# Output projection with three weight slots and passes of 2, 3 and 3 token tiles; the first product's high parts ahead, TensorE kept busy before it

## The chip, the core and the metric
One core of one Trainium2 chip runs the whole program. The metric is the device time of one execution in microseconds (us), median of the runs; lower is better.

## The reference, cut to what matters
One encoder layer on 1024 tokens of width 1024, in float32:
```
x = x + 0.5 * rmsnorm((silu(h @ w1_gate) * (h @ w1_up)) @ w1_down, g)      # h = rmsnorm(x)
z = rmsnorm(x) @ w_in                                                       # pool channels, q, k, v
a = concat(pool_mixer(z), dilated_window_attention(z))                      # 1024 tokens x 1024
x = x + rmsnorm(a @ w_out, g_mix_post)                                      # the output projection
x = x + 0.5 * rmsnorm((silu(h @ w2_gate) * (h @ w2_up)) @ w2_down, g)       # h = rmsnorm(x)
```

## The kernel before
Every large product splits each float32 operand into a high part (rounded to fp32r, made by ScalarE with a copy) and a low part (the rest, made by VectorE with a subtraction), and adds three products on TensorE: high by high, high by low, low by high. So each weight piece passes ScalarE, then VectorE, then TensorE. The engines run fixed instruction lists written by hand, each in its own order, joined by semaphore waits; a wait in one list holds all that stands behind it in that list.

Stages, in order: gate/up of the first feed-forward half (`gate_up(0)`), its down product (`down(0)`), input projection with attention, output projection (`project_out`), `gate_up(1)`, `down(1)`. A token tile is 128 tokens; there are NT = 8, four to a half (HT).

**Start of a gate/up stage.** Tiles 0 to 3 are normalised (`x_norm`), turned by TensorE (`turn_x`, 8 transposes), and their turned form is split: `x_hi` and `x_copy` on ScalarE, `x_lo` on VectorE. Three tail products (`tail_product`, X, Y and Z, 24 matmuls of 128x512 each) come first; their weights are split by `hi_tail` and `lo_tail`. Between them TensorE turns tiles 4 to 7 (`turn_second`), which VectorE takes apart in `split` (one subtraction in two pieces, then two sums) and `s_14` (two more sums). Then come the 12-matmul products (`product`) in the order of FIRST_M: (0,0), (1,0), (0,4), (1,4), where the first number is the weight unit, and after them three more tail products, which need all four `split`. The weights of unit 0 and 1 are 1 MB loads by SyncE, which start once `lo_tail` of Y and of Z are done. `first_steps` holds these lists for ScalarE and VectorE.

**End of a gate/up stage.** `combine` and `times_up` on VectorE finish the stage, `lo_d(0)` and `lo_d(1)` make the low parts of the first two steps of the down product; TensorE's first down step waits for `lo_d(0)`.

**Output projection.** For a pass of token tiles, TensorE runs 8 units, one for each 128 rows of `w_out`; a unit is 6 matmuls of 128x512 for each tile of the pass. The passes are `OUT_TILES`, (0,1,2), (3,4,5), (6,7): 18, 18 and 12 matmuls a unit. For each unit `hi_proj` (ScalarE, 128x1024 and 128x384 or 128x256) and `lo_proj` (VectorE, the same shapes) split weights and activations, into one of two slots; a slot is free when the unit two before is done. In the first pass the activations are only just made: TensorE turns the attention's output (`turn_outputs`), ScalarE and VectorE copy it. Before unit 1 the softmax coefficients go through TensorE, and GpSimd scales the outputs with them (`scale_out`, L518).
Beside the units, each finished tile i takes a chain of small steps, whose places in the order `OUT_SIDE` fixes (the unit index n is counted through all 24): copy out of PSUM (`evac_mix`), square sum (`sq1`), GpSimd's root, `scale_y` and `x_new` on VectorE, store and next load and `sq2` on ScalarE, GpSimd's root, `x_norm` on VectorE, and for tiles 0 to 3 `turn_x`, `x_hi`, `x_copy`, `x_lo`:
```
OUT_SIDE = {7: 0, 10: 1, 13: 2, 16: 3, 18: 4, 20: 5}
...
for base, i in OUT_SIDE.items():
    if n == base:
        sq1(R_MIX + i, junk_f[:, :], mixed)
    if n == base + 2:
        x_store(R_MIX + i)
        x_load(R_MIX + i + 2)
        sq2(Q_FFN[1] + i, junk_f[:, :])
```
`x_store` waits on ScalarE for `x_new` of its tile. Tiles 6 and 7 are left for `last_mixed`.

## Time and profile before
| | |
|---|---|
| median of 3 runs | 1762.67 us (1762.55 to 1763.8) |
| the profiled execution | 1763.64 us, its span 1761.2 us |
| TensorE busy | 1708.9 us, 97% of the span |
| VectorE, ScalarE, GpSimd busy | 1117.0, 711.6, 628.6 us |
| mean granted TensorE clock | 0.991 |

The span runs from the first to the last instruction; the rest of the execution, 2.4 us, lies around it. An engine's busy time counts the union of its instructions.

### The profile page before, as it was taken

What the parts mean: (1) busy time and instruction counts of PE and PEld (TensorE: products, weight loads), DVE (VectorE), ACT (ScalarE), POOL (GpSimd) and SP (SyncE); (2) the same over time, 40 slices, a digit from 0 to 9 for tenths busy, and PEclk for the clock granted to TensorE, in tenths of its full rate; (3) what the DMA queues carried; (4) which work ended last, traced back from release to release, by engine and by line L of the source; (5) the groups of instructions that cost most, each with busy time, mean ns of one, the idle gap of its engine ahead of it and who ended that gap; (6) DMA issues with size and microseconds to landing.
All of it is one profiled execution on the core that took longest, in us unless ns stands there. A gap on an engine that the chain in (4) does not pass through costs nothing.

```text
span 1761.2 us, 21622 instructions
## 1 busy us (share of the span) xinstructions
PE 1708.9 (97%) x7918; PEld 1403.7 (80%) x7918; DVE 1117.0 (63%) x1403; ACT 711.6 (40%) x1256; POOL 628.6 (36%) x494
## 2 busy tenths in 40 slices
PE   6999999999999999999999999899999999999997
PEld 5888888888788878887888787688888888788886
DVE  6775665565668784424556658877665655557877
ACT  6433323332444553433444456533333333244453
POOL 3354554553453111108010201246554544445111
PEclk8999999999999999999999899999999999999999
DMA  6142224323853445332110156422233233384362
GB/s 209 42 133 95 90 91 130 115 90 104 315 186 98 142 150 162 113 97 84 49 50 23 49 167 202 130 87 90 90 111 135 90 104 104 141 294 147 101 228 90
DMA packets 160984, 216.97 MB, mean 123 GB/s; under 512 B 12848, under 2 KB 99056, under 8 KB 160880
## 3 DMA queue, kind: packets, MB, share of 16 engines
q1 hardware_dynamic: 153136, 188.73, 33.6%
q10 hardware_dynamic: 6896, 24.19, 3.9%
q0 software_dynamic: 848, 2.69, 0.5%
q8 instruction: 63, 1.03, 0.2%
q14 instruction: 41, 0.34, 0.1%
HBM read 162.09 MB, written 52.95 MB: 122 GB/s over the span
## 4 chain that ended last, share of the span: by engine, by line
PE 88%; DVE 6%; ACT 3%; issue 2%; POOL 1%; ACTq 0%; DMA 0%; DVEq 0%; POOLq 0%
PE ps L1960 15%; PE ps L1959 14%; PE ps L1961 14%; PE ps L2022 7%; PE ps L2024 7%; PE ps L2023 7%; PE ps L2052 4%; PE ps L2054 4%; PE ps L2053 4%; PE ps L2162 2%; PE ps L2270 1%; PE ps L2272 1%; PE ps L2271 1%; PE ps L2130 1%; PE ps L1917 1%
## 5 line engine op out<-in xcount | busy, mean ns | idle before, releaser
L1960 PE MATMUL ps<-xg,ring 128*128 128x512 f32 x1120 | 440.1, 393 | 0.0
L1959 PE MATMUL ps<-xg,ring 128*128 128x512 f32 x1120 | 437.7, 391 | 2.0 <-DVE u_a L1280 1.8
L1961 PE MATMUL ps<-xg,ring 128*128 128x512 f32 x1120 | 437.8, 391 | 0.0
L1959 PEld LDWEIGHTS ps<-xg,ring 128*128 128x128 f32 x1120 | 210.2, 188 | 51.3 <-DVE ring L1140 2.2
L1960 PEld LDWEIGHTS ps<-xg,ring 128*128 128x128 f32 x1120 | 210.4, 188 | 45.0
L1961 PEld LDWEIGHTS ps<-xg,ring 128*128 128x128 f32 x1120 | 210.4, 188 | 44.7
L2022 PE MATMUL ps<-ring 128*128 128x512 f32 x616 | 240.6, 391 | 2.7 <-DVE ring L1152 2.7
L2023 PE MATMUL ps<-ring 128*128 128x512 f32 x616 | 239.8, 389 | 0.0
L2024 PE MATMUL ps<-ring 128*128 128x512 f32 x616 | 239.7, 389 | 0.0
L683 ACT ACTIVATE ring<-t_sum 128x512 fp32r<-128x512 f32 x160 | 100.4, 630 | 290.1 <-PE ps L1961 162.1
L1159 DVE TENSOR_TENSOR ring<-raw,ring 128x1024 fp32r<-128x1024 f32 x64 | 84.6, 1322 | 154.8 <-ACT ring L705 129.7
L1673 POOL TENSOR_TENSOR t_sum<-raw 128x512 f32<-128x512 f32 x80 | 112.9, 1431 | 148.0 <-DVE ring L1140 132.2
L1140 DVE TENSOR_TENSOR ring<-t_sum,ring 128x512 fp32r<-128x512 f32 x160 | 151.5, 956 | 21.3 <-ACT ring L683 21.3
L1640 POOL TENSOR_SCALAR ms<-ss 128x1 f32<-128x1 f32 x44 | 20.7, 471 | 349.4 <-ACT junk_d L742 113.1
L1695 POOL TENSOR_TENSOR u_a<-hst 128x512 f32<-128x512 f32 x40 | 66.4, 1659 | 204.5 <-DVE hst L1269 204.5
L2022 PEld LDWEIGHTS ps<-ring 128*128 128x128 f32 x616 | 115.6, 188 | 28.5 <-DVE ring L1152 4.7
L1149 DVE TENSOR_TENSOR ring<-st_op,ring 128x1024 fp32r<-128x1024 f32 x66 | 103.9, 1575 | 51.3 <-ACT ring L694 51.1
L2024 PEld LDWEIGHTS ps<-ring 128*128 128x128 f32 x616 | 115.6, 188 | 24.1
L2023 PEld LDWEIGHTS ps<-ring 128*128 128x128 f32 x616 | 115.6, 188 | 23.9
L1140 DVE TENSOR_TENSOR ring<-raw,ring 128x512 fp32r<-128x512 f32 x120 | 126.6, 1055 | 5.7 <-ACT ring L683 5.7
L2052 PE MATMUL ps<-xe,ring 128*128 128x512 f32 x320 | 128.6, 402 | 0.0
L2054 PE MATMUL ps<-xe,ring 128*128 128x512 f32 x320 | 125.6, 393 | 0.0
(209 smaller groups left out, 2795.1 us busy)
## 6 DMA issues: line engine op xcount, KB each, us to landing
st_op<-hd_dram SPq DMA_DIRECT2D x154, 256.0 KB, 2.6
raw<-in_w_gate_dram SPq DMA_DIRECT2D x20, 1024.0 KB, 6.5
raw<-in_w_up_dram SPq DMA_DIRECT2D x20, 1024.0 KB, 5.4
raw<-in_w_in_dram SPq DMA_DIRECT2D x40, 512.0 KB, 3.9
hd_dram<-u_b SPq DMA_DIRECT2D x64, 256.0 KB, 6.4
wd<-in_w_down_dram SPq DMA_DIRECT2D x18, 768.0 KB, 7.3
hd_dram<-hst SPq DMA_DIRECT2D x48, 256.0 KB, 6.4
raw<-in_w_out_dram SPq DMA_DIRECT2D x24, 512.0 KB, 3.6
```

What stands on the lines that cost most here:

```text
L683: act.activation(small(m % RING, 0), src, ACT.Copy).then_inc(hi_done, 4 if m == M_FRONT - 1 else 1)
L1140: dve.tensor_tensor(small(m % RING, 1), src, small(m % RING, 0).bitcast(F32), ALU.subtract)\
L1149: a = dve.tensor_tensor(lo, src, hi.bitcast(F32), ALU.subtract)
L1673: pool.tensor_tensor(t_tile(n, t), x, y, ALU.subtract).then_inc(t_done, 1)
L1959: pe.matmul(acc, hi[:, a, :], x_hi, start=(a == 0 and not more), stop=False, skip_group_check=more)
L1960: pe.matmul(acc, hi[:, a, :], x_lo, start=False, stop=False, skip_group_check=more)
L1961: mm = pe.matmul(acc, lo[:, a, :], x_hi, start=False, stop=(a == HALF_D - 1), skip_group_check=more)
L2022: pe.matmul(acc, s_hi, w_hi, start=(j == 0 and not top), stop=False, skip_group_check=top)
L2023: pe.matmul(acc, s_hi, w_lo, start=False, stop=False, skip_group_check=top)
L2024: return pe.matmul(acc, s_lo, w_hi, start=False, stop=(j == PAIRS - 1), skip_group_check=top)
L2052: pe.matmul(ps[:, bank, :], hi[:, a, :], x_hi, start=(a == 0), stop=False)
L2054: mm = pe.matmul(ps[:, bank, :], lo[:, a, :], x_hi, start=False, stop=(a == DT - 1))
```

## The change
1. The start: VectorE makes all four norms before the first `x_lo`; ScalarE puts the tail weights between tiles and all but one `x_copy` behind; TensorE gets 6, 8, 3 and 14 extra transposes of the identity into unused banks (`fill`). Tail product X runs as 8 high by high matmuls, 8 low by high, 8 high by low, waiting for the low parts only where they come in; its first wait is for high parts alone. Other PSUM banks go with it.
2. Both `first_steps`: on VectorE `split(0)` moves behind `lo_g(1)`, and all `s_14` behind `lo_g(5)`; product (1,0) on TensorE now waits for `split(1)`.
3. Both ends of gate/up: `lo_d(0)` and `lo_d(1)` move ahead of `combine(4)`.
4. The output projection: passes (0,1), (2,3,4), (5,6,7), three slots instead of two, tables of places in place of `OUT_SIDE`; three tiles instead of two are left to `last_mixed`; the tail weights X and Y are split by ScalarE before the last unit. GpSimd starts the loads of the two gains after the last attention values instead of the last scores. For buffers this costs g_post_r and g_pre_r new places in SBUF (72 and 76 KB).

```diff
@@ -60,7 +60,7 @@
...
-TAIL_BANK = {(X_T, 0): 5, (Y_T, 0): 4, (Z_T, 0): 5, (Z_T, 1): 1, (X_T, 1): 5, (Y_T, 1): 1}
+TAIL_BANK = {(X_T, 0): 7, (Y_T, 0): 6, (Z_T, 0): 7, (Z_T, 1): 1, (X_T, 1): 5, (Y_T, 1): 1}
@@ -81,7 +81,7 @@
...
-TURN1_BANK, TURN2_BANK = (4, 0, 2, 6), (2, 6, 2, 6)
+TURN1_BANK, TURN2_BANK = (6, 0, 2, 4), (2, 0, 2, 6)
@@ -115,7 +115,7 @@
...
-OUT_TILES = [(0, 1, 2), (3, 4, 5), (6, 7)]
+OUT_TILES = [(0, 1), (2, 3, 4), (5, 6, 7)]
@@ -131,7 +131,12 @@
...
-OUT_SIDE = {7: 0, 10: 1, 13: 2, 16: 3, 18: 4, 20: 5}
+OUT_SQ1, OUT_NEW, OUT_SQ2 = (7, 9, 16, 17, 19), (8, 10, 17, 18, 20), (9, 11, 18, 19, 21)
+OUT_NORM, OUT_TURN = (10, 12, 19, 20, 22), (12, 14, 21, 22)
+EARLY = len(OUT_SQ1)
+FILL, FILL_BANK = (6, 0, 8, 3, 14), (5, 5, 5, 5, 6)
@@ -399,7 +404,7 @@
...
-            return (u - IN_U0[0]) % 2
+            return (u - IN_U0[0]) % 2 if u < OUT_U0 else (u - OUT_U0) % 3
@@ -701,10 +703,17 @@
...
                 act.wait_ge(p_loaded[k % RAW_SLOTS], 16 * (k // RAW_SLOTS + 1))
-                act.wait_ge(used, D0[0] + D_STEPS - 2 + k if k < 2 else u - 1)
+                if u < OUT_U0 + 2:
+                    act.wait_ge(used, D0[0] + D_STEPS - 2 + k if k < 2 else u - 1)
+                elif u == OUT_U0 + 2:
+                    act.wait_ge(pool_step, POOL_STEPS)
+                    act.wait_ge(s_done, NTILES)
+                else:
+                    act.wait_ge(used, u - 2)
                 a = act.activation(big(out_slot(u), 0), raw[:, k % RAW_SLOTS, :], ACT.Copy)
                 if src is not None:
-                    a = act.activation(hs_out[0][:, k % 2, 0:src.shape[-1]], src, ACT.Copy)
+                    a = act.activation(hs_out[0][:, out_slot(u), 0:src.shape[-1]], src, ACT.Copy)
                 a.then_inc(hi_done, 1)
@@ -1063,30 +1075,31 @@
...
-                    for base, i in OUT_SIDE.items():
-                        if n == base:
+                    for i in range(HT):
+                        if n == OUT_TURN[i]:
+                            x_hi(Q_FFN[1] + i, 6)
+                            x_copy(Q_FFN[1] + i, 6)
+                    for i in range(EARLY):
+                        if n == OUT_SQ1[i]:
...
-                        if n == base + 2:
+                        if n == OUT_SQ2[i]:
...
-                        if i < HT and n == base + 5:
-                            x_hi(Q_FFN[1] + i, 6)
-                            x_copy(Q_FFN[1] + i, 6)
-                    if n == 3 * OUT_UNITS - 3:
-                        hi_tail(1, X_T)
+                    if n >= 3 * OUT_UNITS - 3:
+                        hi_tail(1, n - 3 * OUT_UNITS + 3)
...
-                sq1(R_MIX + 6, junk_f[:, :], mixed)
-                sq1(R_MIX + 7, junk_f[:, :], mixed)
-                hi_tail(1, Y_T)
+                for i in range(EARLY, NT):
+                    sq1(R_MIX + i, junk_f[:, :], mixed)
...
-                x_store(R_MIX + 6)
-                sq2(Q_FFN[1] + 6, junk_f[:, :])
-                x_store(R_MIX + 7)
-                sq2(Q_FFN[1] + 7, junk_f[:, :])
+                for i in range(EARLY, NT):
+                    x_store(R_MIX + i)
+                    if i + 2 < NT:
+                        x_load(R_MIX + i + 2)
+                    sq2(Q_FFN[1] + i, junk_f[:, :])
@@ -1100,15 +1113,17 @@
...
             for i in range(HT):
-                if i == HT - 1:
+                if i == 2:
                     hi_tail(0, X_T)
                 x_hi(i, TURN1_BANK[i])
-                if i < HT - 1:
-                    x_copy(i, TURN1_BANK[i])
+                if i == 0:
+                    x_copy(0, TURN1_BANK[0])
             hi_tail(0, Y_T)
+            x_copy(1, TURN1_BANK[1], late=True)
             sq2(4, junk_0[:, 4, :])
+            x_copy(2, TURN1_BANK[2], late=True)
+            sq2(5, junk_0[:, 5, :])
             x_copy(3, TURN1_BANK[3], late=True)
-            sq2(5, junk_0[:, 5, :])
             sq2(6, junk_0[:, 6, :])
@@ -1281,23 +1295,21 @@
...
                 lo_g(p, 0)
-                split(p, 0)
-                s_14(p, 0)
                 lo_g(p, 1)
                 tail_times_up(p, Y_T, 0)
+                split(p, 0)
                 lo_g(p, 2)
                 split(p, 1)
-                s_14(p, 1)
                 lo_g(p, 3)
...
                 split(p, 2)
-                s_14(p, 2)
                 lo_g(p, 4)
                 split(p, 3)
-                s_14(p, 3)
                 lo_g(p, 5)
+                for i in range(HT):
+                    s_14(p, i)
+                lo_g(p, 6)
                 s_lo(p, OP_S3)
-                lo_g(p, 6)
                 lo_g(p, 7)
@@ -1338,6 +1350,8 @@
...
                             times_up(p, n, 1)
+                        if m == M_STEPS - 2:
+                            lo_d(p, 1)
                         if k == 5:
@@ -1346,9 +1360,8 @@
...
                                 times_up(p, n, 3)
-                        if m == M_STEPS - 2:
+                        if m == M_STEPS - 3:
                             lo_d(p, 0)
-                            lo_d(p, 1)
                         m += 1
@@ -1560,27 +1573,25 @@
...
-                    for base, i in OUT_SIDE.items():
-                        if n == base + 1:
+                    for i in range(EARLY):
+                        if n == OUT_NEW[i]:
...
-                        if n == base + 3:
+                        if n == OUT_NORM[i]:
...
-                        if i < HT and n == base + 5:
+                        if i < HT and n == OUT_TURN[i]:
...
-                x_norm(Q_FFN[1] + 5, g_pre_r)
+                lo_tail(1, Y_T)
...
-                scale_y(R_MIX + 6, g_post_r)
-                lo_tail(1, Y_T)
-                scale_y(R_MIX + 7, g_post_r)
-                x_new(R_MIX + 6)
-                x_new(R_MIX + 7)
+                for i in range(EARLY, NT):
+                    scale_y(R_MIX + i, g_post_r)
+                    x_new(R_MIX + i)
...
-                x_norm(Q_FFN[1] + 6, g_pre_r)
-                x_norm(Q_FFN[1] + 7, g_pre_r)
+                for i in range(EARLY, NT):
+                    x_norm(Q_FFN[1] + i, g_pre_r)
@@ -1606,9 +1617,10 @@
...
                 x_norm(i, g_pre_r)
-                if i:
-                    x_lo(i - 1, TURN1_BANK[i - 1], copied=True)
+            x_lo(0, TURN1_BANK[0], copied=True)
+            x_lo(1, TURN1_BANK[1])
             lo_tail(0, X_T)
+            x_lo(2, TURN1_BANK[2])
             x_lo(3, TURN1_BANK[3])
@@ -1860,20 +1872,26 @@
+            def fill(i):
+                for _ in range(FILL[i]):
+                    pe.transpose(ps[:, FILL_BANK[i], 0:P], ident[:, :], ident[:, :])
-                if i >= 2:
+                if i == 3:
+                    pe.wait_ge(tail_act, 6 * p + 3)
+                    pe.wait_ge(tail_done, 4 * p + 1)
+                elif i == 2:
                     pe.wait_ge(xlo_done, q - 1)
                 elif p == 0:
-                    pe.wait_ge(xlo_done, 3 + i)
-                    pe.wait_ge(xcopy_done, 3 + i)
-                elif i == 0:
-                    pe.wait_ge(mix_act, NT)
-                    pe.wait_ge(mix_dve, NT)
+                    pe.wait_ge(xlo_done, 3 - i)
+                    pe.wait_ge(xcopy_done, 3 - i)
                 else:
-                    pe.wait_ge(xlo_done, Q_FFN[1] + HT)
+                    pe.wait_ge(mix_act, 7 - i)
+                    pe.wait_ge(mix_dve, 7 - i)
                 src = xn_tile(p, HT + i)
@@ -1885,9 +1903,11 @@
...
-                if half == 0:
+                if s == 0:
+                    pe.wait_ge(hi_done, G0[p] + 1)
+                    pe.wait_ge(xhi_done, Q_FFN[p] + HT)
+                elif half == 0:
...
-                    pe.wait_ge(xlo_done, Q_FFN[p] + HT)
@@ -1895,22 +1915,29 @@
...
                     else:
-                        pe.wait_ge(mix_act, 6)
-                        pe.wait_ge(mix_dve, 6)
+                        pe.wait_ge(xlo_done, Q_FFN[1] + HT)
+                        pe.wait_ge(xcopy_done, 2 * HT)
                 elif s == 2:
                     pe.wait_ge(tail_act, 6 * p + 1)
-                elif s == 7:
-                    if p == 0:
-                        pe.wait_ge(xcopy_done, 2)
-                    else:
-                        pe.wait_ge(mix_act, NT)
-                        pe.wait_ge(mix_dve, NT)
-                elif s == 8:
-                    pe.wait_ge(tail_act, 6 * p + 3)
-                else:
+                elif s == 9:
                     pe.wait_ge(tail_act, 6 * p + 5)
...
                 hi, lo = (tail_w[t][:, part, :].rearrange("p (a f) -> p a f", a=DT) for part in (0, 1))
+                if s == 0:
+                    for a in range(DT):
+                        x_hi = xg[:, (OP_A11, OP_A12)[a // HALF_D], 0, a % HALF_D, :]
+                        pe.matmul(acc, hi[:, a, :], x_hi, start=(a == 0), stop=False)
+                    pe.wait_ge(lo_done, G0[p] + 1)
+                    for a in range(DT):
+                        x_hi = xg[:, (OP_A11, OP_A12)[a // HALF_D], 0, a % HALF_D, :]
+                        pe.matmul(acc, lo[:, a, :], x_hi, start=False, stop=False)
+                    pe.wait_ge(xlo_done, Q_FFN[p] + HT)
+                    for a in range(DT):
+                        x_lo = xg[:, (OP_A11, OP_A12)[a // HALF_D], 1, a % HALF_D, :]
+                        mm = pe.matmul(acc, hi[:, a, :], x_lo, start=False, stop=(a == DT - 1))
+                    mm.then_inc(used, 1)
+                    return
                 for a in range(DT):
@@ -1928,13 +1955,13 @@
...
                     if (n, k) == (0, 0):
-                        pe.wait_ge(tail_done, 4 * p + 1)
-                    if (n, k) == (1, 0):
                         if p == 0:
-                            pe.wait_ge(xcopy_done, 2)
+                            pe.wait_ge(xcopy_done, HT)
                         else:
...
                             pe.wait_ge(mix_dve, NT)
+                    if (n, k) == (1, 0):
+                        pe.wait_ge(xlo_done, Q_FFN[p] + HT + 2)
                     if (n, k) == (0, 1):
@@ -2252,19 +2279,19 @@
...
                         turn_outputs(n + 2)
-                    for base, i in OUT_SIDE.items():
-                        if i < HT and n == base + 6:
+                    for i in range(HT):
+                        if n == OUT_TURN[i]:
                             turn_x(Q_FFN[1] + i, 6)
...
                     pe.wait_ge(lo_done, u + 1)
-                    b, k = out_slot(u), (u - IN_U0[0]) % 2
+                    b = out_slot(u)
                     for m in range(len(tiles)):
-                        if l == 0 and part:
+                        if l == 0 and part and m < len(OUT_TILES[part - 1]):
                             i = OUT_TILES[part - 1][m]
...
                             pe.wait_ge(mix_dve, i + 1)
-                        hi, lo = (h[:, k, m * P:(m + 1) * P] for h in hs_out)
+                        hi, lo = (h[:, b, m * P:(m + 1) * P] for h in hs_out)
                         for c in (0, 1):
@@ -2276,7 +2303,12 @@
...
             for i in range(HT):
+                fill(i)
                 turn_x(i, TURN1_BANK[i])
+            pe.wait_ge(xlo_done, 1)
+            pe.wait_ge(xcopy_done, 1)
+            fill(HT)
             gate_up(0)
```

**The order on the engines.** TensorE from its first instruction, before and now (ident is the identity, y the normalised tokens, tail_w a tail weight, xg the turned tokens):
```order
L1859 MATMUL ps<-ident,y 128x128 x32
L1917 MATMUL ps<-xg,tail_w 128x512
L1918 MATMUL ps<-xg,tail_w 128x512
L1919 MATMUL ps<-xg,tail_w 128x512
L1917 MATMUL ps<-xg,tail_w 128x512
L1918 MATMUL ps<-xg,tail_w 128x512
```
```order
L1878 MATMUL ps<-ident 128x128 x6
L1871 MATMUL ps<-ident,y 128x128 x16
L1878 MATMUL ps<-ident 128x128 x8
L1871 MATMUL ps<-ident,y 128x128 x8
L1878 MATMUL ps<-ident 128x128 x3
L1871 MATMUL ps<-ident,y 128x128 x8
L1878 MATMUL ps<-ident 128x128 x14
L1930 MATMUL ps<-xg,tail_w 128x512 x8
L1934 MATMUL ps<-xg,tail_w 128x512 x8
L1938 MATMUL ps<-xg,tail_w 128x512 x8
L1897 MATMUL ps<-ident,y 128x128 x8
L1944 MATMUL ps<-xg,tail_w 128x512
```
Transposes of the identity stand between the turns, and product X is three runs of eight instead of a mix.

VectorE at the head of `first_steps(0)`, before and now (L1140/L1155 `lo_g`, L1280/L1294 tail gate times up, L1208 to L1213 and L1222 to L1227 `split`, L1218 and L1219 `s_14`):
```order
L1140 TENSOR_TENSOR ring<-raw,ring 128x512
L1208 TENSOR_TENSOR xg<-ps,xg 128x4x128 x2
L1211 TENSOR_TENSOR y<-y,ps 128x512
L1213 TENSOR_TENSOR y<-ps,y 128x512
L1218 TENSOR_TENSOR y<-y 128x512
L1219 TENSOR_TENSOR y<-y 128x512
L1140 TENSOR_TENSOR ring<-raw,ring 128x512
L1280 TENSOR_TENSOR u_a<-ps,u_a 128x512
L1140 TENSOR_TENSOR ring<-raw,ring 128x512
L1208 TENSOR_TENSOR xg<-ps,xg 128x4x128 x2
L1211 TENSOR_TENSOR y<-y,ps 128x512
L1213 TENSOR_TENSOR y<-ps,y 128x512
```
```order
L1155 TENSOR_TENSOR ring<-raw,ring 128x512 x2
L1294 TENSOR_TENSOR u_a<-ps,u_a 128x512
L1222 TENSOR_TENSOR xg<-ps,xg 128x4x128 x2
L1225 TENSOR_TENSOR y<-y,ps 128x512
L1227 TENSOR_TENSOR y<-ps,y 128x512
L1155 TENSOR_TENSOR ring<-raw,ring 128x512
L1222 TENSOR_TENSOR xg<-ps,xg 128x4x128 x2
L1225 TENSOR_TENSOR y<-y,ps 128x512
L1227 TENSOR_TENSOR y<-ps,y 128x512
L1155 TENSOR_TENSOR ring<-raw,ring 128x512
L1294 TENSOR_TENSOR u_a<-up_rows,u_a 64x512
```
The first `split` now stands behind the second weight piece, and `s_14` has left the place between the splits.

VectorE at the end of a gate/up stage, before and now (L1253/L1267 and L1255/L1269 `combine`, L1269/L1283 `times_up`, L1151 and L1152, now L1166 and L1167, `lo_d`):
```order
L1269 TENSOR_TENSOR hst<-ps,sil 128x512
L1269 TENSOR_TENSOR hst<-m1b,sil 128x512
L1253 TENSOR_TENSOR uu<-uu,ps 128x512
L1269 TENSOR_TENSOR hst<-uu,sil 128x512
L1151 TENSOR_TENSOR ring<-st_op,ring 128x512
L1152 TENSOR_TENSOR ring<-wd,ring 128x512
L1151 TENSOR_TENSOR ring<-st_op,ring 128x512
L1152 TENSOR_TENSOR ring<-wd,ring 128x512
L1255 TENSOR_TENSOR uu<-ps,uu 128x512
L1269 TENSOR_TENSOR hst<-uu,sil 128x512
```
```order
L1283 TENSOR_TENSOR hst<-ps,sil 128x512
L1283 TENSOR_TENSOR hst<-m1b,sil 128x512
L1166 TENSOR_TENSOR ring<-st_op,ring 128x512
L1167 TENSOR_TENSOR ring<-wd,ring 128x512
L1166 TENSOR_TENSOR ring<-st_op,ring 128x512
L1167 TENSOR_TENSOR ring<-wd,ring 128x512
L1267 TENSOR_TENSOR uu<-uu,ps 128x512
L1283 TENSOR_TENSOR hst<-uu,sil 128x512
L1269 TENSOR_TENSOR uu<-ps,uu 128x512
L1283 TENSOR_TENSOR hst<-uu,sil 128x512
```
Two `lo_d` have moved ahead of two `combine` and two `times_up`.

## Rows read from the trace of the kernel before
**Rows 1.** The page: busy time, share of the span, instructions, by engine.
```profile
PE 1708.9 (97%) x7918; PEld 1403.7 (80%) x7918; DVE 1117.0 (63%) x1403; ACT 711.6 (40%) x1256; POOL 628.6 (36%) x494
```

**Rows 2.** Waits of TensorE: line, who ended them, us in total, times, longest.
```profile
PE ps L2022 <- DVE ring L1152: 2.7, 4, 1.1
```

**Rows 3.** Timeline, start: start us, us, engine, line, operation, names, shapes, count, [idle before <-releaser].
```profile
9.89 3.88 PE L1859 MATMUL ps<-ident,y 128*128 128x128 f32 x16 [9.89 <-DVE y L1188]
...
11.88 0.55 POOL L1642 TENSOR_TENSOR r<-ms,neg_half 128x1 f32<-128x1 f32 x1
...
23.46 0.77 PE L1917 MATMUL ps<-xg,tail_w 128*128 128x512 f32 x1 [2.60 <-issue]
...
31.10 1.03 PE L1879 MATMUL ps<-ident,y 128*128 128x128 f32 x8
```

**Rows 4.** Windows: stretch, length, busy us by engine, granted clock, DMA share, GB/s.
```profile
14.30:17.60 3.30, 1.10 (x8) 0.86 (x8) 3.30 (x6) 1.51 (x3) 0.00 (x0) 1.00 1.15 330
...
17.70:27.80 10.10, 6.31 (x18) 5.08 (x19) 7.77 (x9) 9.78 (x16) 2.67 (x5) 0.50 0.63 220
...
1096.30:1099.60 3.30, 3.30 (x10) 2.42 (x9) 3.27 (x3) 0.00 (x0) 0.00 (x0) 0.50 0.59 156
```

**Rows 5.** Timeline of the first half's start, ScalarE, VectorE, SyncE's queue, TensorE.
```profile
27.87 1.06 ACT L665 ACTIVATE tail_w<-raw 128x1024 fp32r<-128x1024 f32 x1
...
30.22 0.38 SPq L542 DMA_DIRECT2D raw<-in_w_up_dram  x1
...
34.74 1.27 DVE L1208 TENSOR_TENSOR xg<-ps,xg 128x512 fp32r<-128x512 f32 x2
...
35.77 0.63 ACT L683 ACTIVATE ring<-raw 128x512 fp32r<-128x512 f32 x1 [2.00 <-DMA raw<-in_w_up_dram]
...
47.32 0.48 PE L1959 MATMUL ps<-xg,ring 128*128 128x512 f32 x1
...
56.55 0.39 PE L1917 MATMUL ps<-xg,tail_w 128*128 128x512 f32 x1
```

**Rows 6.** Timeline where the first gate/up stage meets its down stage.
```profile
446.26 1.77 DVE L1152 TENSOR_TENSOR ring<-wd,ring 128x512 fp32r<-128x512 f32 x1
...
448.09 0.50 PE L2022 MATMUL ps<-ring 128*128 128x512 f32 x1 [1.12 <-DVE ring L1152]
```

**Rows 7.** Timeline of the output projection's first pass.
```profile
1003.89 7.21 POOL L518 TENSOR_TENSOR vT<-vT,coef 128x2048 f32<-128x2048 f32 x2 [2.51 <-DVE coef L1453]
...
1008.03 4.15 DVE L1159 TENSOR_TENSOR ring<-raw,ring 128x1024 fp32r<-128x1024 f32 x1 [0.44 <-ACT mhi L707]
...
1012.70 0.50 PE L2270 MATMUL ps<-ring,mhi 128*128 128x512 f32 x1 [0.42 <-DVE mlo L1162]
...
1017.01 1.03 PE L2242 MATMUL ps<-ident,vT 128*128 128x128 f32 x8
...
1021.19 0.55 DVE L1162 TENSOR_TENSOR mlo<-mixT,mhi 128x384 fp32r<-128x384 f32 x1
...
1040.62 0.46 PE L2270 MATMUL ps<-ring,mhi 128*128 128x512 f32 x1
```

**Rows 8.** Timeline of its last pass.
```profile
1095.14 0.50 PE L2270 MATMUL ps<-ring,mhi 128*128 128x512 f32 x1 [1.81 <-DVE mlo L1162]
...
1097.45 1.28 DVE L1179 SCALAR_TENSOR_TENSOR y<-y,r,x_buf 128x1024 f32<-128x1024 f32 x1
...
1099.70 1.06 ACT L763 ACTIVATE junk_f<-y 128x1024 f32<-128x1024 f32 x1 [4.92 <-DVE y L1179]
```

**Rows 9.** Timeline from its end into the second half.
```profile
1107.69 0.39 PE L2272 MATMUL ps<-ring,mlo 128*128 128x512 f32 x1
...
1124.69 0.37 SPq L542 DMA_DIRECT2D raw<-in_w_up_dram  x1
...
1131.97 0.63 ACT L683 ACTIVATE ring<-raw 128x512 fp32r<-128x512 f32 x1 [3.38 <-DMA raw<-in_w_up_dram]
...
1148.38 0.39 PE L1917 MATMUL ps<-xg,tail_w 128*128 128x512 f32 x1
```

31 lines of the change are left out of this document (15 added, 16 removed).

## The prediction
> **What bounds the kernel.** The page comes first: TensorE is busy 97% of the span [rows 1], so a change that leaves its work alone can win only where it stands still or runs at half clock. The work does stay: the passes hold 18+18+12 matmuls before and 12+18+18 now, eight times each, and 31 small transposes are added in front. Next come TensorE's waits, a view that names the ends of its gaps; one of them is the down weight's low part [rows 2]. The timeline then shows each gap, and the windows the clock. Four places hold what this change touches:
> - The first real matmul starts at 23.46, its product is over at 31.10 [rows 3]; the granted clock is 0.50 from 17.7 to 27.8 [rows 4].
> - TensorE waits 1.12 us for `lo_d(0)` where gate/up meets down [rows 6].
> - The output projection's first pass runs nearly closed: from 1012.70 to 1040.62 [rows 7].
> - Its later passes wait for low parts, 1.81 at 1095.14, behind ScalarE, which itself stood 4.92 for `x_new` at 1099.70 [rows 8]; then the next half starts with gaps [rows 9].
>
> **Start: -4.7 us.** The third tile's root is ready at 11.88 + 0.55 = 12.4 [rows 3]. Now nothing stands between the norms on VectorE; at 1.28 us each the third ends at 13.8 and the fourth, its root held some 1.3 us while VectorE is busy, at 15.7. The turns follow at 14.9 and 16.1, ScalarE's fourth `x_hi` ends at 18.1, the 14 fillers (0.11 each at full clock, 0.24 cold: 3.88 / 16 [rows 3]) at 18.6. Product X starts there instead of at 23.46. Its 8 high by low matmuls need `x_lo(3)`: four 1.2 us pieces and `lo_tail(X)` end at 21.7, in time. At 0.228 a matmul, 24 take 5.5: it ends at 24.1, which is 7.0 early.
> That lead can't be kept. Product (1,0) now waits for `split(1)`. `hi_tail(Z)` stays where it was, at 27.87 + 1.06 [rows 5], since ScalarE has the same work ahead of it; I reckon 27.8. `lo_tail(Z)` 29.0, load of unit 1 landed 5.5 later (30.22 to 35.77 [rows 5]) at 34.6, `hi_g(1)` 35.2, `lo_g(1)` 36.0, then 0.6 + 2.6 + 0.6 + 2.6 (a `split` is 1.27 for its two pieces [rows 5] and two sums of 0.7) for the four VectorE steps up to `split(1)`: 42.5. TensorE without waits would be there at 24.1 + 0.8 + 5.5 + 0.8 + 5.5 + 2.8 + 0.8 = 40.3 and stands 2.2. It starts at 42.6 where before it was at 47.32 [rows 5]: **4.7** gained. The rest of the stage is closed: `split(3)` ends at 50.1 against 51.8 wanted (56.55 before [rows 5]), and the eight sums moved behind it (4.9) are out before product (0,3) at 68. Nothing is late next.
> What the fillers are worth: two turns and 17 fillers at half clock instead of full would put ScalarE's fourth `x_hi`, and the whole chain behind it to `split(1)`, 2.5 us later. The trace speaks for them: the clock was granted in full from 14.3 to 17.6 [rows 4] though nothing but 16 transposes had run [rows 3]. The Trainium skill, TensorE: Matmul & The Clock Gate, Part 4, says the opposite: full clock "doesn't engage for transpose-mode (it doesn't count as PE-busy the same way)"; by that rule the start would gain 2.2 in place of 4.7. The rows contradict it, so it is a rival with a small chance.
>
> **Ends of gate/up: -3.3 us.** `lo_d(0)` ends at 446.26 + 1.77 [rows 6], released only after `combine(4)`. Ahead of it, it is done by about 445, before the last matmul ends at 446.8. The gap of 1.3 goes, and with it a 0.4 one at the third step; the waits for this line are 2.7 in four [rows 2], and with the issue delay around them 3.3. What moves back (`combine(4)`, `times_up`) frees banks that TensorE wants only 11 steps on, and stores that are read ten steps on: nothing. The bound below is 1.5, if `lo_d(2)` becomes late behind them with GpSimd's 1.77 us contention.
>
> **Output projection, first pass: +2.2 us.** Two tiles make a unit 12 x 0.233 = 2.8 instead of 4.2. Unit 0 ends 1.4 earlier, and the coefficients and GpSimd's scaling (1003.89, 7.21 long [rows 7]) with it: that ends at 1009.8. VectorE's low part of unit 2 took 4.15 and ended 1.1 after GpSimd did [rows 7]; it still will: unit 2 starts at 1011.35, not 1012.70, though 2.8 us of work have gone from ahead of it. After that a unit needs its chain: from the turn at 1017.01 to the low part at 1021.19 + 0.55 is 4.73 [rows 7], some 0.2 less with 256 columns instead of 384. TensorE offers 2.8 + 0.8 + 0.8 = 4.4 while turns go on, and 2.8 + 0.8 for unit 6: waits of 0.15 and 0.95. The second pass starts at 1031.65; 1040.62 [rows 7] less the 11.2 us moved behind it is 1029.4. Loss 2.2.
>
> **Later passes: -5.4 us.** Before, from 1040.62 to the end at 1107.69 + 0.23 [rows 9], 67.3 us, for 56.0 of matmuls and four turns of 0.8: 59.2. So 8.1 lost, part of it at granted clock 0.50 (1096.3 to 1099.6 [rows 4]). Now the third slot lets ScalarE start a unit one unit (4.2) earlier; a wait of 4.92 for `x_new` is then nearly covered. Going through ScalarE's and VectorE's lists with 1.5 for a high part, 1.65 for a low, 2.5 for `scale_y` and `x_new` (1.28 each [rows 8]), 2.1 from `x_new` to the end of `sq2`, 0.9 for a root, all low parts come in time, but two turns don't: the one before unit 14 waits 1.1 for `x_norm(1)`, which stands behind `x_lo(0)`, and the one before unit 22 waits 1.5 for `x_lo(2)`, behind `new(4)`, `norm(3)` and `lo(23)`. 2.6 in place of 8.1: 5.5, rounded down. The projection ends at 1104.7, counted on the old clock of this stretch.
>
> **Into the second half: -5.1 us.** Before, 40.5 us from 1107.9 to product (Z, 1) at 1148.38 [rows 9]. Now tail X follows at once, its parts being ready. Tile 5 to 7's chain is in order: three `sq1` to 4.6 after the end, `x_new(7)` 9.9, `lo_tail(Z)` 11.1, `x_norm(5)` 12.4 (the second turn waits 0.6), `silu` 13.6 (tail Z waits 0.4). Unit 1's load takes 7.3 here (1124.69 to 1131.97 [rows 9]), lands at 18.4; the same chain as in front puts `split(1)` at 26.2. TensorE waits 3.4 there in two pieces; product (Z, 1) starts at 35.3. 40.5 - 35.3 = 5.2, rounded to 5.1.
>
> GpSimd's two gain loads, moved behind the last attention values, still start some 50 us before `x_new` wants them: nothing, and a late one would show as a wait of GpSimd.
>
> **Sum.** -4.7 - 3.3 + 2.2 - 5.4 - 5.1 = -16.3 on the profiled execution's 1763.64 (span 1761.2, 2.4 around it, taken as constant): 1747.3. The median is 1.0 below that execution, so I forecast 1746.5. A difference of 0.2% or 3.5 us can be told from none.
>
> **Rivals.**
> - *Transposes don't hold the clock* (5%): the first product starts cold, all before `split(1)` 2.5 later: 1749. It is what the page cited above would have; rows 4 speak against it.
> - *The clock falls elsewhere* (15%): new short stands of 1 to 2.4 us before unit 2, before turns, before (1,0) bring stretches at 0.50, as the gap of 1.81 at 1095.14 did [rows 4, 8]. A stretch costs 1.6 (10 matmuls in 3.3 us [rows 4] for 14); two to four of them: 1749.5 to 1753. Against it: the gaps before were longer, and the mean clock was still 0.991.
> - *The stands I reckon don't come* (17%): VectorE's pieces overlap by 0.1 each and my order walk is the late side; without the two turn waits (2.6), unit 6's (1.0) and half of the 2.2 and 3.4: 1740 to 1743.
> - *The ring is not what bound the later passes* (6%): VectorE's chains eat the third slot, and 5.4 shrinks to 0: 1752 to 1755.
> - *Slower* (2%): `split` on the path. Product (1,0) now hangs on ten VectorE steps in either half. If GpSimd's sums run beside them, each takes 1.77 instead of 0.68 [rows 6]: 10 x 1.1 x 2 = 22 us, 1768. It decides from 8 contended steps a half on. Against it: GpSimd's four sums there wait for `lo_g(4)`, which stands behind.
> - *It doesn't do what it says* (1%): the waits go elsewhere, 1760 to 1763.
>
> The forecast itself has 54%, with its own range 1743.5 to 1749.5. The 80% range takes in the first three rivals: 1740 to 1752.5. Faster 0.96, same 0.02, slower 0.02.
>
> **What would show it.** First tail matmul near 18.6, three runs of eight, clock 1.00 from 14 on; a stand of 1 to 3 us before product (1,0) in both halves, ended by `split`. No wait for `lo_d`. Unit 2 of the first pass right after GpSimd; later passes closed but for two turns; tail X without a gap after the last unit. A clock of 0.50 in front, or low parts still waited for after unit 8, would prove me wrong.

## The result, and the profile after

The changed kernel took 1754.96 us (median of 5 runs, 1752.69 to 1755.39), the kernel before 1763.8 in the same session (1762.55 to 1764.78). The ratio of the runs is 0.9948, 95% interval 0.9935 to 0.9961. It is faster, as forecast, but by 8.8 us where my sum had 16.3, and the time lies outside my range, which ended at 1752.5. The profiled execution took 1755.16, its span is 1753.3.

I compare the two profiles by the place of the same matmul in each. All times are us from the span's start:

| stretch | before | after | change | forecast |
|---|---|---|---|---|
| start to the first down matmul | 448.09 | 441.88 | -6.2 | -6.0 |
| from there to the output projection | 544.6 | 546.3 | +1.7 | -0.35 |
| output projection | 115.2 | 115.0 | -0.2 | -3.2 |
| from its end to the second down matmul | 432.0 | 428.5 | -3.5 | -6.4 |
| from there to the end of the span | 221.3 | 221.6 | +0.3 | -0.35 |
| sum | 1761.2 | 1753.3 | -7.9 | -16.3 |

(The forecast's 3.3 for the ends of gate/up is split here: 1.3 before and 0.35 behind the first down matmul, in each half.) The first row came as reckoned, the other four did not. The page's first line still shows a busy TensorE:
```profile
PE 1709.8 (98%) x7949; PEld 1406.1 (80%) x7949; DVE 1116.9 (64%) x1403; ACT 712.0 (41%) x1256; POOL 635.4 (36%) x494
```
Its timeline at the start answers to [rows 3, 5]: fillers (L1878), the turns, product X in three runs of eight, and product (1,0) ended by `split`.
```profile
9.62 3.98 PE L1871 MATMUL ps<-ident,y 128*128 128x128 f32 x16
...
16.83 1.75 PE L1878 MATMUL ps<-ident 128*128 128x128 f32 x14
...
18.33 2.09 PE L1930 MATMUL ps<-xg,tail_w 128*128 128x512 f32 x8
...
41.12 0.47 PE L1986 MATMUL ps<-xg,ring 128*128 128x512 f32 x1 [0.71 <-DVE y L1227]
```
Product X starts at 18.33 (forecast 18.6, before 23.46), product (1,0) at 41.12 (42.6, before 47.32).

TensorE's waits (columns: line, who ended them, us in total, times, longest), without the 8.1 in which the first filler waits for the identity's load:
```profile
PE ps L1871 <- DVE y L1388: 3.1, 1, 3.1
PE ps L1871 <- DVE xg L1212: 2.8, 1, 2.8
PE ps L1986 <- DVE y L1227: 2.7, 2, 2.0
PE ps L2297 <- DVE mlo L1177: 2.6, 2, 1.9
PE ps L1944 <- ACT hst L820: 2.0, 2, 1.0
PE ps L1897 <- DVE y L1202: 1.6, 1, 1.6
PE ps L2049 <- DVE ring L1167: 1.4, 2, 0.7
```
The first shown is an old one, at a turn inside the down product. The second is the turn before unit 22, the fourth mostly unit 2 of the first pass. The fifth I had not foreseen at all: tail product (Y,1) in both halves. The last answers to [rows 2]: 2.7 in four became 1.4 in two, at the third down step.

Below, a stand is time in which TensorE stands still, and a stretch is time at half clock. The granted clock in three windows (stretch of time, length, busy us by engine, clock, DMA share, GB/s):
```profile
631.80:635.20 3.40, 3.40 (x11) 2.73 (x10) 3.40 (x6) 1.09 (x2) 0.00 (x0) 0.50 0.24 74
1007.30:1010.70 3.40, 3.40 (x10) 2.63 (x9) 1.61 (x3) 0.00 (x0) 0.00 (x0) 0.50 0.70 175
1130.20:1133.50 3.30, 3.30 (x9) 2.63 (x8) 3.27 (x6) 0.00 (x0) 0.00 (x0) 0.50 0.02 5
```
In such a stretch matmuls start 0.43 apart instead of 0.23, as TensorE's timeline shows at unit 2:
```profile
1007.52 0.63 PE L2297 MATMUL ps<-ring,mhi 128*128 128x512 f32 x1
1007.94 0.63 PE L2298 MATMUL ps<-ring,mhi 128*128 128x512 f32 x1
```
Eight such starts lose 8 x 0.2 = 1.6 a stretch. The first of the three lies in code that the change does not touch. Between the start and the last matmul, both profiles spend the same 17 us at half clock: before at 990.4 (6.8 long), 1004.1, 1096.3 and 1120.2, after at 631.8, 986.8, 997.0, 1007.3 and 1130.1, each 3.4 long. So these stretches did not make the change slower than before; but the forecast had counted those at 1096.3 and 1120.2 as gone and no others as coming.

The new wait of (Y,1), in ScalarE's timeline:
```profile
58.43 0.63 ACT L685 ACTIVATE ring<-t_sum 128x512 fp32r<-128x512 f32 x1 [8.48 <-POOL t_sum L1685]
58.97 2.18 ACT L801 ACTIVATE xg<-y 128x512 fp32r<-128x512 f32 x4
61.05 0.58 ACT L813 ACTIVATE hst<-ps 64x512 f32<-64x512 f32 x1
61.65 0.59 ACT L820 ACTIVATE hst<-ps 64x512 f32<-64x512 f32 x1
```
and what TensorE did meanwhile:
```profile
61.02 0.39 PE L1946 MATMUL ps<-xg,tail_w 128*128 128x512 f32 x1
62.39 0.47 PE L1944 MATMUL ps<-xg,tail_w 128*128 128x512 f32 x1 [0.98 <-ACT hst L820]
```
ScalarE gets the sum for `hi_g(7)` from GpSimd only at 58.4 (GpSimd took 3.48 for it, from 54.86 on, while VectorE made four low parts), then makes four high parts for S1, one of the two sums of `s_14` (2.18), and only then the silu and copy that free bank 1 for (Y,1).

And the turn before unit 22: VectorE makes `x_lo(2)`, which the turn waits for, behind the low part of unit 23.
```profile
1090.89 1.22 DVE L1174 TENSOR_TENSOR ring<-raw,ring 128x1024 fp32r<-128x1024 f32 x1
...
1092.03 0.55 DVE L1177 TENSOR_TENSOR mlo<-mixT,mhi 128x384 fp32r<-128x384 f32 x1
1092.49 1.28 DVE L1212 TENSOR_TENSOR xg<-ps,xg 128x512 fp32r<-128x512 f32 x2
...
1093.92 0.85 PE L1871 MATMUL ps<-ident,y 128*128 128x128 f32 x6 [2.79 <-DVE xg L1212]
```

### The profile page after: what moved, and what is told of

The parts are those of the page before. It is cut to its first block, busy times and chain, and to the rows that moved or that the text cites. A ratio compares the mean times of both kernels' runs of the same rounds, so it can differ in the third digit from the quotient of the medians.

```text
span 1753.3 us, 21676 instructions
## 1 busy us (share of the span) xinstructions
PE 1709.8 (98%) x7949; PEld 1406.1 (80%) x7949; DVE 1116.9 (64%) x1403; ACT 712.0 (41%) x1256; POOL 635.4 (36%) x494
## 4 chain that ended last, share of the span: by engine, by line
PE 83%; DVE 6%; issue 4%; ACT 3%; POOL 1%; DMA 1%; ACTq 0%; POOLq 0%; DVEq 0%
PE ps L1986 14%; PE ps L1987 14%; PE ps L1988 14%; PE ps L2049 7%; PE ps L2051 7%; PE ps L2050 7%; PE ps L2079 4%; PE ps L2081 4%; PE ps L2080 4%; PE ps L2189 2%; PE ps L2157 1%; PE ps L1871 1%; PE ps L2297 1%; POOL t_sum L1685 1%; PE ps L2172 1%
## 5 line engine op out<-in xcount | busy, mean ns | idle before, releaser
L1685 POOL TENSOR_TENSOR t_sum<-raw 128x512 f32<-128x512 f32 x80 | 117.2, 1484 | 146.2 <-DVE ring L1155 129.8
L1155 DVE TENSOR_TENSOR ring<-t_sum,ring 128x512 fp32r<-128x512 f32 x160 | 151.6, 957 | 20.8 <-ACT ring L685 20.8
L1155 DVE TENSOR_TENSOR ring<-raw,ring 128x512 fp32r<-128x512 f32 x120 | 127.4, 1062 | 5.5 <-ACT ring L685 5.5
```

Source lines behind the costliest of these rows:

```text
L1155: dve.tensor_tensor(small(m % RING, 1), src, small(m % RING, 0).bitcast(F32), ALU.subtract)\
L1685: pool.tensor_tensor(t_tile(n, t), x, y, ALU.subtract).then_inc(t_done, 1)
```

## The experiments

Sixteen kernels ran. All but e14 were timed in five rounds against the kernel before, whose medians in these sessions were 1763.8 to 1766.96; I compare the kernels by their own medians, with e1 as the changed kernel's. Runs of one kernel can lie far apart (e1: 1754.02 to 1761.74), and the rounds ran on three different chips. Against the kernel before, the 95% intervals of e3, e5, e6, e8 and e16 stand clear of e1's (0.9933 to 0.9964); those of e2, e4, e7, e9 to e13 and e15 overlap it, so that for these the place of the same matmul in the traces has to bear out the median.

**e1: the changed kernel again.**

> The changed kernel once more, nothing edited. Theory A (the half-clock stretches follow the stands of TensorE): they lie at the same five places as in the profile of after (631.8, 986.8, 997.0, 1007.3, 1130.1), each some 3.4 us long, and the times agree within 0.1%. Rival B (they come at random): places differ from one profile to the next, and the times of the runs, 1752.7 to 1755.4 so far, lie apart by whole stretches of 1.6 us.

1755.02. Four of the five places agree (632.1, 987.1, 997.4, 1130.5), the stretch at 1007.3 was absent and one at 1092.9 came, behind the stand of the turn before unit 22. So it is neither A nor B: these two each follow a stand, but which stand gets one differs from profile to profile. The profiled run took 1761.74; what its trace shows of that is told at the end.

**e2: silu of (Z,1) first, e3: tile 4 one unit later, e5: both.**
```diff
# e2, ScalarE
-                s_hi(p, OP_S1)
                 silu_tail(p, Z_T, 1)
+                s_hi(p, OP_S1)
# e3
-OUT_SQ1, OUT_NEW, OUT_SQ2 = (7, 9, 16, 17, 19), (8, 10, 17, 18, 20), (9, 11, 18, 19, 21)
+OUT_SQ1, OUT_NEW, OUT_SQ2 = (7, 9, 16, 17, 19), (8, 10, 17, 18, 21), (9, 11, 18, 19, 22)
```


> ScalarE's silu of tail Z's second half stands ahead of the four sums' high parts s_hi(S1). In after the tail product (Y,1) stood 1.14 us at 61.0 and 1.15 us at 1150.9 for that silu's copy. Theory A (ScalarE's order is the wait): both stands go, 2.2 us less than e1, 1752.5 or so. Rival B (ScalarE is late as a whole, behind GpSimd's sum and VectorE's eight sums): the stand moves to the next step that needs s_hi(S1), gain under 0.5 us.

> VectorE's scale_y and x_new of mixed tile 4 one unit later (unit 21 instead of 20), its squares with it (22). In after the turn before unit 22 stood 2.8 us for x_lo(2), which ended behind new(4) (2.5 us). Theory A (order of VectorE's list): that stand shrinks to 0.3 or less, 1.5 to 2.8 us less than e1, as nothing wants tile 4 before the second half's turns. Rival B: the load of tile 6 starts a unit later, x_new(6) and the second half's first turns come later by as much, and the time is that of e1 within 0.5 us.

> Both orders together: silu of (Z,1) ahead of the high parts of S1, and tile 4's x_new one unit later. Theory A (both were waits of their own on TensorE): e1 1755.0 less 3.0 (e2) less 5.2 (e3) = 1746.8, about what I had forecast for the change. Rival B (part of e3's 5.2 was half-clock stretches that happened not to fall, as its profile had none at 1130): 1755.0 - 2.2 - 2.8 = 1750.

e2: 1752.04, 3.0 less; both stands of (Y,1) are gone from its profile, in which the start comes out 1.2 shorter than in after and the way into the second half 1.1. e3: 1749.84, 5.2 less; the turn before unit 22 waits 0.34 instead of 2.79:
```profile
1090.76 1.06 PE L1871 MATMUL ps<-ident,y 128*128 128x128 f32 x8 [0.34 <-DVE xg L1212]
```
Its profile lacks two of after's stretches, those at 986.8 and 1130, which is where it gained more than the stand. e5: 1747.62 (1747.5 to 1749.35), 7.4 less than e1: nearest to A. Its ratio to the kernel before is 0.9904 (0.9888 to 0.992), clear of the change's 0.9948. It is the best kernel of the study, and beats both.

**e4 and e6: transposes in the stands.** e4 has three places, of which I misplaced one: the 26 went in at a turn of the input projection (675.8 in its profile), which does not wait, and cost 2.8 there, 26 x 0.11. e6 is e5 with three places.
```diff
+                    if n == 2:
+                        hold(16, 5)          # e6, e13: 12
                     pe.wait_ge(lo_done, u + 1)
...
+                if p == 1 and (n, k) == (1, 0):
+                    hold(17, 5)              # e6: 7 and 15 in both halves; e13: 15
                 pe.wait_ge(lo_done, g_step(p, n, k))
```


> Small transposes into a free bank while TensorE would stand still: 26 before the turn at 627.9 (wait 3.05), 16 before unit 2 of the output projection (wait 1.94), 17 before product (1,0) of the second half (wait 2.00). They add no wait, since they fit into those. Theory A (a stand brings the half clock behind it, transposes hold it off): the stretches at 631.8, 1007.3 and 1130.1 are gone, the granted clock there 1.00, and the time is 3 x 1.6 = 4.8 us less than e1. Rival B (what decides is not whether TensorE is busy in the stand): the stretches stay or turn up elsewhere, the time is e1's, or up to 1 us more.

> e5 with small transposes into bank 5 in three stands: 12 before unit 2 of the output projection (stand 1.9), 7 and 15 before product (1,0) of the first and second half (stands 0.7 and 2.0). In the profile of e4 the clock stayed 1.00 behind those at unit 2 and (1,0) and its time was still e1's, but 2.5 us of that were 26 transposes that I had put at a turn of the input projection which does not wait. Theory A (a stand brings a half-clock stretch, 1.6 us): 1 to 3 us less than e5, no stretch at 1007 or 1130. Rival B (the stretches only move on to other stands): within 0.5 us of e5.

e4: 1754.96, with no stretch behind either held stand; that is e1's time in spite of the 2.8. e6: 1747.98, e5's time. e5 itself had no stretch at 1007 or 1130 in its profile, though it stood 1.5 and 2.0 there, so the holds had nothing to win. That left the question to e13.

**e13: two holds, nothing else.**

> The changed kernel with 12 small transposes before unit 2 of the output projection and 15 before product (1,0) of the second half, where after stood 1.9 and 2.0 and the clock fell behind both; nothing else (e4 without its misplaced 26). Theory A (these two stretches are in most runs and are the price of the stands): 2 x 1.6 = 3.2 less than e1: 1751.8 to 1752.5. Rival B (the stretches come and go with the run whether held or not): within 0.7 of e1, 1754.3 to 1755.7.

1753.61, 1.4 less than e1: between A and B. The clock held where I held it, and fell behind the stand of 2.8 that I had left alone:
```profile
1006.00:1009.40 3.40, 3.21 (x18) 2.52 (x17) 3.28 (x5) 1.35 (x3) 0.00 (x0) 1.00 0.39 106
1094.50:1097.80 3.30, 3.30 (x11) 2.62 (x10) 0.74 (x2) 2.85 (x4) 0.00 (x0) 0.50 0.03 7
1130.00:1133.40 3.40, 3.03 (x16) 2.35 (x14) 3.40 (x6) 0.33 (x1) 0.00 (x0) 1.00 0.02 5
```
Two held stands are worth 1.4 on the median, not 3.2, and 1.4 is hardly clear of the noise; its profile, at 1753.0, is no shorter than after's, since a stretch at 630.3 is twice as long there and the one at 1094.5 is new.

Part of the reason lies in the profiles with nothing in these stands. Of the ten that stood 2.0 or more before product (1,0) of the second half, six have a stretch behind it (after, e1, e2, e7, e10, e12) and four have none (e3, e5, e8, e11). At unit 2, the four that stood 1.9 to 2.8 have one (after, e3, e7, e16), and the six that stood 1.3 to 1.7 have none (e1, e2, e5, e10, e11, e12). In the three kernels with transposes there (e4, e6, e13) neither place has one.

**e14: the kernel before again.**

> The kernel before once more, for a second profile. At the turn in the down product TensorE stood 3.05 in the profile of before (end at 636.94) with no half-clock stretch behind it, in after there was one (631.8). Theory A (that stretch is an accident of the profiled run, and no part of the change): this profile may have it, and the span of down and input projection is 1.6 longer than the first profile's. Rival B (the change brought it): none here either.

1762.96. Rival B: no stretch behind the stand in this profile either, and its others lie where before had them (990.4, 1004.0, 1096.2, 1120.1). Of the sixteen profiles with the change in them, 14 have a stretch at some 630 to 636; e4 and e8 have none. The stand is the same in both kernels. Here it is in the timeline of before again, in that of e4, and e4's window behind it:
```profile
636.86 1.09 PE L1860 MATMUL ps<-ident,y 128*128 128x128 f32 x8 [3.06 <-DVE y L1376]
```
```profile
631.10 1.09 PE L1871 MATMUL ps<-ident,y 128*128 128x128 f32 x8 [3.06 <-DVE y L1388]
```
```profile
632.00:635.40 3.40, 3.40 (x20) 2.81 (x19) 3.40 (x6) 1.49 (x3) 0.00 (x0) 1.00 0.28 66
```
Two profiles of before without and 14 of 16 with it speak for an effect of the change (the stand now comes 6 us earlier), though the two profiles of before have all their stretches at the same places within 0.1 and so say little more than one; what decides is open.

**e7: no fillers.** `FILL = (0, 0, 0, 0, 0)`.

> The changed kernel without its 31 fillers in front; nothing else. Theory A (transposes keep the clock up): the turns and product X run at clock 0.50 at first, the chain to split(1) and product (1,0) is about 2.5 us later, product (1,0) at 43.6 instead of 41.1; 1757.5. Rival B (transposes do nothing for the clock, the early product does it all): as e1, 1755.

1754.78, the time of e1: rival B for the time, but not for its reason. Product X starts at 18.11, as early as with fillers, and at full clock. Its timeline:
```profile
9.72 3.70 PE L1871 MATMUL ps<-ident,y 128*128 128x128 f32 x16 [9.72 <-DVE y L1202]
13.64 1.09 PE L1871 MATMUL ps<-ident,y 128*128 128x128 f32 x8 [0.21 <-DVE y L1202]
15.64 1.09 PE L1871 MATMUL ps<-ident,y 128*128 128x128 f32 x8 [0.91 <-DVE y L1202]
18.11 1.16 PE L1930 MATMUL ps<-xg,tail_w 128*128 128x512 f32 x4 [1.38 <-DVE xg L1212]
```
and in the windows:
```profile
13.20:30.00 16.80, 14.23 (x73) 11.37 (x72) 14.53 (x17) 16.60 (x26) 8.23 (x12) 1.00 0.83 253
```
Transposes do bring the clock up, since nothing else had run by 13.2; but the sixteen of the first two turns are enough, and it stays up over stands of 1.4 and less. Before, the clock fell at 17.6 [rows 4], behind a stand of 2.7 between the turns:
```profile
16.50 1.10 PE L1859 MATMUL ps<-ident,y 128*128 128x128 f32 x8 [2.73 <-DVE y L1188]
```
That the shorter stands come from the norms in a row is by the lists; it was not run alone. The Trainium skill, TensorE: Matmul & The Clock Gate, Part 4, has transposes not count towards full clock; these rows contradict it a second time, if `pe.transpose` is that mode: the trace calls it MATMUL.

**e10: product X in the old order.** The three runs of eight are mixed again, behind `lo_done` and `xlo_done`.

> Product X in the old order (high and low parts mixed, all of it waits for x_lo(3) and lo_tail(X)). Theory A (high parts first starts TensorE early, but split(1) binds): product X starts near 20.6 instead of 18.3, product (1,0) at 42.4 instead of 41.1, since its wait of 0.98 takes up the rest: 1.3 us more than e1, 1756.3. Rival B (split(1) is behind product X on the chain as well): 2.3 more, 1757.3. Rival C (a stand of 2.3 before X brings the clock down to 0.50 as in the kernel before, where X took 7.6): 3 to 4 more.

1757.19 (1754.96 to 1763.53), 2.2 more; rival C is what the profile shows. Fillers end, TensorE stands, and the clock falls on product X (timeline, then the window):
```profile
16.82 1.75 PE L1878 MATMUL ps<-ident 128*128 128x128 f32 x14
21.58 0.47 PE L1929 MATMUL ps<-xg,tail_w 128*128 128x512 f32 x1 [3.02 <-issue]
```
```profile
23.10:26.30 3.20, 3.20 (x9) 2.51 (x8) 2.00 (x2) 3.20 (x6) 2.81 (x4) 0.50 0.76 219
```
The first down matmul comes 3.8 later than in after. Product X starts 3.25 later and takes 1.6 longer by the stretch; the stand before product (1,0), 1.0 in after, takes up the rest. So it is the order of product X that keeps TensorE and its clock going in front, not the fillers.

**e11: `lo_d` back behind `combine(4)`.**

> The first two low parts of the down weight back to where they were, behind combine(4). Theory A (they were the wait at the turn from gate/up to down): stands of 1.1 to 1.3 at 446 and 1537 come back, but the 0.8 of after at the third down step goes, as the traces of before and after had it: 1.9 more than e1, 1756.9. Rival B: under 0.5, the time only moved from the first down step to the third.

1755.58, 0.56 more, though its profile has both stands back (2.7 in four, word for word [rows 2] but for the lines) and loses 1.3 and 1.2 at them against after, of which it wins back 0.4 at each third step. It has one stretch fewer than after (none at 1007 or 1130, one at 1094), 1.6. The order is worth 1.9 by its stands, 0.6 by the medians.

**e12: the sums `s_14` back between the splits.**

> The eight sums s_14 back between the splits. Theory A (VectorE's list sets product (1,0)): two sums of 0.7 and one more before split(1): product (1,0) at 42.5 to 43.2 instead of 41.1 and likewise in the second half; but lo_g(6), GpSimd's sum behind it and with them the silu before (Y,1) come earlier, so that the 1.14 us at 61.0 and 1150.9 shrink: net 1 to 2 us more than e1, 1756 to 1757. Rival B (the sums only trade one stand for the other): the time of e1 within 0.5.

1754.73: rival B. Product (1,0) starts 1.3 later (42.40), (Y,1) gains 0.85 of that back in either half. Moving eight VectorE sums bought a stand's removal and made another.

**e8: two slots.** `out_slot` takes `% 2` everywhere, the high part waits for `used` of the unit before.

> The changed kernel with two weight slots in the output projection instead of three, passes and tables as they are. Theory A (the third slot closed the later passes): TensorE again waits for low parts L1177 behind x_new, some 1.8 us at several units, and the projection ends 3 to 6 us later: 1758 to 1761. Rival B (the ring did not bind, the new tables did it): 1755 to 1756.

1765.01, 10 more than e1: the time of the kernel before. The projection takes 127.5 instead of 115.0. Theory A's direction holds and its price was too low; the stands are turns rather than units' low parts:
```profile
PE ps L1864 <- DVE y L1195: 5.2, 4, 1.9
PE ps L1864 <- DVE xg L1205: 5.0, 1, 5.0
```

**e9 and e15: passes of 3, 3 and 2 with three slots.**
```diff
-OUT_TILES = [(0, 1), (2, 3, 4), (5, 6, 7)]
+OUT_TILES = [(0, 1, 2), (3, 4, 5), (6, 7)]
-OUT_NORM, OUT_TURN = (10, 12, 19, 20, 22), (12, 14, 21, 22)
+OUT_NORM, OUT_TURN = (10, 13, 16, 19, 21), (12, 15, 18, 21)    # e15: (12, 15, 19, 21)
```


> The changed kernel with its three weight slots but passes of 3, 3 and 2 tiles, and the side work of a tile at the steps it had before (tile 5's chain behind the passes). e8 showed 10 us for the third slot under passes 2, 3, 3. Theory A (slots close the later passes whatever the tiles): the loss of the first pass (2.2 by my sum) is gone and the later passes are closed too; the last pass of two tiles starves by its chain, 4.7 per unit against 2.8 to 3.6: 6 us or more; 1757 to 1761. Rival B (the third slot is all): within 1 us of e1, 1755.

> e9 (passes 3, 3, 2 with three slots, 1752.7) with three small orders: silu of (Z,1) first (2.2 to 3.0 by e2), the third turn before unit 19 instead of 18, where it stood 2.3 for x_norm(2), and x_norm(5) ahead of x_new(7), which waited 1.7 for its load while the second turn of the second half stood 2.9 for x_norm(5). Theory A: 2.5 + 2 + 1 to 2.5 less: 1745.2 to 1747.2, so passes 2, 3, 3 bring nothing that 3, 3, 2 with three slots don't have. Rival B (the last pass of two tiles starves, the stands move on): 1748 to 1750, behind e5's 1747.6.

e9: 1752.71, 2.3 less than the change, of which 1.4 lie in the projection. With the tables as they were first written, the old passes with a third slot beat the new ones; neither theory had that. e15: 1752.85 (1749.11 to 1754.11), nothing won, and neither theory's range. (Y,1) is gone, but the fourth turn and tail Z stand now:
```profile
1093.04 1.97 PE L1873 MATMUL ps<-ident,y 128*128 128x128 f32 x8 [4.63 <-DVE y L1202]
...
1120.15 0.47 PE L1946 MATMUL ps<-xg,tail_w 128*128 128x512 f32 x1 [2.61 <-ACT u_a L813]
```

Put side by side, the projection's length in the traces shows what e8 alone can't:

| | passes 3, 3, 2 | passes 2, 3, 3 |
|---|---|---|
| two slots | 115.2 (before) | 127.5 (e8) |
| three slots | 113.6 (e9), 117.3 (e15) | 115.0 (after), 112.5 (e3), 110.9 (e5) |

The third slot is worth 12.5 under the new passes, but 1.6 under the old ones (e9's side steps stand a little otherwise than before's, so this is rough). The new passes cost 12.3 with two slots and 1.4 with three; the slot mostly pays for them. And one table entry moves more than that 1.4: with tile 4 later, the new passes (e3, 1749.84) are 2.9 ahead of e9. So e9 does not show that the new passes are worse; the best kernel has them, and the one attempt at better tables for the old ones failed. What the passes are worth with the best tables of each is open.

**e16: e5 with `x_norm(5)` ahead of `x_new(7)`.**

> e5 (1747.6) with x_norm(5) ahead of x_new(7) on VectorE. The second turn of the second half stood 1.5 for x_norm(5), and x_new(7) 1.1 for its load. Theory A: that stand goes, and product (1,0) comes earlier by part of it, since split(1) behind the turn comes earlier too: 0.5 to 1.5 less, 1746.1 to 1747.1. Rival B (product (1,0) is bound by unit 1's load and lo_g(1)): the stand moves behind, same time within 0.4.

1749.32, 1.7 more. The second turn's stand went (1.55 gained) and tail Z stood 2.77 for ScalarE's silu, which stands behind the squares of tile 7, later by one norm; a stretch at 1115 came with it. From the projection's end to the down product its profile is 0.4 longer than e5's, so by the trace the stand only moved: rival B. The other 2.0 lie in the projection, ahead of the edit: there unit 2 stood 2.8 instead of 1.5 and had a stretch behind it. e15's 3.7 more in the projection than e9's lie ahead of the same edit too, at the fourth turn.

## Why the prediction missed

The start came out as forecast. What failed is the step from the new lists to TensorE's waits everywhere else: new stands were sized too low or not seen ((Y,1), the third down step, the turn before unit 22, the second turn), and the half-clock stretches stood in the sum at nothing. Part by part:

- **Start, -4.7: right in size, wrong in one reason.** 4.9 was kept. High parts first (e10: 2.2 on the median, 3.8 in the trace) does most of it; I credited the fillers with 2.5, and e7 gives them nothing. The half clock in front was no matter of missing transposes: e7, where no stand is over 1.4, and e10, where the clock falls behind one of 3.0, speak for the stand of 2.7 between the turns. The `split` chain came 1.5 earlier than I reckoned; the unforeseen stand of (Y,1), 1.3, used that up, so the right size is partly luck.
- **Ends of gate/up, -3.3: mis-sized.** The stands of 1.1 went, but a new one of 0.7 (0.86 with issue) stands at the third step in both halves, where I had removed one of 0.4: 1.9 in the trace. It is the bound I named ("`lo_d(2)` becomes late") nearly reached.
- **First pass and later passes, -3.2 together: 0.2 in the trace.** Two terms make up the difference. Unit 2 started as reckoned (18.4 behind the projection's start, forecast 18.7), but its stand brought a stretch, which I had at nothing: the second pass started at 40.5 instead of 39.0, and at 38.8 in e1, which has no such stretch. The turn before unit 22 stood 2.8 for `x_lo(2)`, not 1.5: the later passes lost 4.1, not 2.6. e3 shows that this was a matter of one unit in a table. The mechanism was half right: three slots do save the later passes, but e8 and e9 show that they save them mostly from the new passes. I charged these with 2.2, in the first pass alone, and never priced slot and passes apart.
- **Into the second half, -5.1: 2.3.** The second turn stood 1.6 for `x_norm(5)`, not 0.6, since `x_new(7)` waited 1.14 for its load, which I left out; product (1,0) stood 2.0 where I had 3.4, but brought a stretch; (Y,1) stood 1.15. e2 shows that (Y,1) is ScalarE's order: I had costed the sums `s_14` against product (0,3) only ("nothing is late next"), not against `lo_g(6)`, GpSimd's sum behind it and ScalarE behind that.
- **The clock, a rival at 15% with 2 to 4 stretches: it happened, three of them, beside the four waits.** My reason against it (the mean clock was still 0.991 before) was no reason: before has as much half clock behind the start, and I let two of its stretches go with their stands without asking which new stands bring one. The price of 1.6 was right, but not my working for it: 10 matmuls in place of 14 would be 0.9; it follows from starts 0.43 apart. The third stretch lies at an old stand in untouched code, and I had no term for that.

So the forecast of 1746.5 was the time of a kernel without these stands. e5, which removes two of them by reordering, is at 1747.6, but that does not confirm the sum. In its profile the start and the projection are 1.4 and 1.1 shorter than forecast, the part between them 2.5 longer; the errors nearly cancel.

Not run alone: the four norms in a row, and the later loads of the two gains.

## What to carry to other kernels

When a sum of work moves on one engine's list, follow the engines behind it until the chain reaches TensorE again, bank by bank: the first consumer of the moved result is not the one that gets late. Price a stand of some 2 us with a share of a half-clock stretch (here 1.6 whole; a bit more than half of such stands had one), and count the stretches that the kernel before has already. Test the parts of a change alone and also in pairs: the slot looked like 10 by taking it away, but the old passes had little use for it; the fillers were worth nothing; and one entry in a table of places was worth more than slot and passes together.
